# The opening of a fused two-block kernel: which queue and which engine prepare the first operands, and where the first norm factor is made

## The chip, the cores and the metric

The kernel runs on one NeuronCore of a Trainium2 chip. The metric is device time in microseconds (us) of one execution. The kernel before takes 1455.27 us, the median of three runs (1454.86 to 1456.52). The names of the engines in the profile are PE (TensorE, with its weight loads as PEld), DVE (VectorE), ACT (ScalarE), POOL (GpSimd) and SP (SyncE, which only issues transfers here).

## The reference

One sequence of 512 positions passes through two layers of width 1024. The change touches only the start of the first one:

```
h = rms_norm(x, g_mix)             # x * rsqrt(mean(x*x) + 1e-6) * g_mix
proj = h @ w_in                    # 1024 x 4352
u_a = proj[..., :1280]             # conv of 4 taps, two-way RG-LRU, @ p_a
u_b = proj[..., 1280:2304]         # pooled means, block-diagonal map, @ p_b
gates = sigmoid(proj[..., 2304:] + b_gate)
x = x + (gates[..., :1024] * y_a + gates[..., 1024:] * y_b) @ w_out
# then rms_norm, w_up, conv of 3 taps, gelu gate, w_down, and the second layer
```

Everything is float32. Channels lie on the 128 partitions and the 512 positions along the row, so x is eight tiles of 128x512.

## The kernel before, in words

**Three passes for each product.** A float32 operand is split into a rounded half "hi" and the remainder "lo". A block of the product (128 input channels times 128 output channels, 512 positions) is three matmuls: hi weights on hi data (L725), lo weights on hi data (L726), hi weights on lo data (L728). The function `block` (L715 to L731) issues them.

**Units of weights.** The weights lie in memory in the order of use, in units of eight blocks (128x1024, 512 KB). A unit goes through four steps: a load into `raw` (SP's queue, or ACT's for unit 1), the rounded half `whi` (ACT, L1222), the negative remainder `wlo` (ACT, L1231), and an accumulating transfer on GpSimd's queue that adds `raw` to it (L2544). For units 0, 1 and 2 VectorE makes the remainder instead, by one subtraction (`remainder`, L1730). `raw`, `whi` and `wlo` each have four slots.

**The first product starts before the norm is known.** The first four output tiles (two of the LRU's input, two of the pooled branch) are computed from v1 = x * g_mix, without the factor 1/rms, by `first`: for each of eight input tiles kk, one block of each of the four outputs. So units 0 to 3 are used up there, two kk to a unit. `gained(m)` (ACT, L1283) makes the hi half of v1's tile m, `gained_rest(m)` (DVE, L1724) the lo half. Both need g_mix, which is the first transfer on ACT's queue (L1275).

**The norm factor.** Squares of x are made on DVE and ACT and added up on DVE. Column sums on TensorE (`sums`, L780, eight small matmuls at a time in the profile) come in two parts: for tiles 0 to 3 after block (3, 1) and for tiles 4 to 7 after block (4, 2); (kk, n) is input tile kk, output n. ACT takes the root (L1246), DVE the reciprocal (L1678), and `to_rows(1)` (L845) after block (5, 0) spreads the factor over 128 partitions with four matmuls. From there DVE makes the normed tiles h1 (L1757), ACT their hi halves (L1307) and DVE their lo halves (L1683). All products behind `first` use h1. Then DVE scales the four outputs of `first` by the factor (L1769) and goes on with the conv and the recurrence.

**Before any operand is there** TensorE multiplies a tile of ones 17 times (`keep_warm_by_ones(17)`, L834), 34 matmul records in the profile.

Each engine runs its list in the order in which it is written, and waits at semaphores; the lists are written out by hand. `Units.due` says at which block a unit is due, which is why `weights(16)` on ACT in the opening stands for unit 4 alone, the first unit behind `first`.

Of the kernel before, what the change touches and what calls it, by code (L numbers as in the profile page):

```python
# [107 lines left out]
class Book:  # L108
# [107 lines left out]
class Kit:  # L216


    def __init__(self, nc, top, x_d, w_d, mod_d, cond_d, vec_d, cst_d, edge_d, ssm_d, uk_d, spill_d,
# [29 lines left out]
        self.gain_in, self.raw_part = sig("gain_in", 16), sig("raw_part", 16)  # L249
# [47 lines left out]
    def sb(self, *name):  # L297
        return self.place(*self.book.home[name])[0]
# [393 lines left out]
def tensor_engine(k, T):  # L692
# [21 lines left out]
    def block(tile, kk, pair, out, start, stop):  # L714

        u, j = divmod(len(k.plan), UB)
        k.plan.append((tile[0], kk, tile[1]))
        c = slice(128 * j, 128 * j + 128)
        wh, wl = k.whi[:, u % NHI, c], k.wlo[:, u % NLO, c]
        if u == 0 and j == 0:  # L720
            T.wait_ge(at("w_hi_part"), at("w_lo_part"))
        elif j == 0 or (u, j) == (0, UB // 2):
            T.wait_ge(at("w_hi", u), at("w_lo", u))
        T.wait_ge(at(pair, kk, "hi"))
        matmul(out, wh, sr(pair, kk, "hi"), start=start, stop=False)  # L725
        matmul(out, wl, sr(pair, kk, "hi"), start=False, stop=False)  # L726
        T.wait_ge(at(pair, kk, "lo"))
        mm = matmul(out, wh, sr(pair, kk, "lo"), start=False, stop=stop)  # L728
        if stop or j == UB - 1:
            mm.then_inc(*done.tick(tile if stop else None))  # L730
        if j == UB - 1:  # L731
            done.note("unit", u)
# [105 lines left out]
    def to_rows(n, copy=None):  # L838
# [5 lines left out]
        for t in range(4):  # L844
# [4 lines left out]


    T.wait_ge(at("ones"))
    keep_warm_by_ones(17)
    first(FIRST_IN, "v1", {(3, 1): lambda: sums([1], 0, last=4), (4, 2): lambda: sums([1], 4, last=4),
                           (5, 0): lambda: to_rows(1)})
    done.release(*[("v1", m, h) for m in range(8) for h in ("hi", "lo")])


# [353 lines left out]
def scalar_engine(k, A):  # L1211
# [22 lines left out]
    def weights(n):  # L1234
        rounded_weights(units.due(n))
# [36 lines left out]
            if m in between:  # L1272
                between[m]()

    A.eng.dma_start(k.vec[:, 0:8], k.vec_d[:, 0:8]).then_inc(*k.gain_in.tick(("gain",)))  # L1275
    A.eng.dma_start(k.raw[:, 0, 0:512], k.w_d[0][:, 0:512]).then_inc(*k.raw_part.tick(("raw_part",)))
    A.eng.dma_start(sb("x0", 1), k.x_d[1]).then_inc(*k.x_in[1].tick(("x0", 1)))
    A.eng.dma_start(k.raw[:, 1, :], k.w_d[1]).then_inc(*k.raw_in[1].tick(("raw", 1)))
    A.eng.preload_act_table(ACT.Sqrt)

    def gained(m):
# [2 lines left out]
            *done.tick(("v1", m, "hi")))  # L1284

    gained(0)
    A.wait_ge(at("raw_part"))
    act(k.whi[:, 0, 0:512], k.raw[:, 0, 0:512], ACT.Copy).then_inc(*k.w_hi.tick(("w_hi_part",)))
    A.wait_ge(at("raw", 0))
    act(k.whi[:, 0, 512:1024], k.raw[:, 0, 512:1024], ACT.Copy).then_inc(*k.w_hi.tick(("w_hi", 0)))  # L1290
    gained(1)
    gained(2)
    rounded_half(1)
    gained(3)
    rounded_weights([2])
    gained(4)
# [1 line left out]
        square(1, m, sb("x0", m), ("x0", m))  # L1298
    rounded_weights([3])
    gained(5)  # L1300
    root(1, 1024)
    gained(6)
    gained(7)
    weights(16)
    for m in range(8):
        A.wait_ge(at("nf", 1, m), *freed("h1", m, "hi"))
        act(sr("h1", m, "hi"), sb("nf", 1, m), ACT.Copy).then_inc(*done.tick(("h1", m, "hi")))  # L1307
        if m in (1, 3):
            weights(8)
# [346 lines left out]
def vector_engine(k, V):  # L1656
# [70 lines left out]
    def remainder(u, cols, raw, hi, lo):  # L1727
# [2 lines left out]
        tt(k.wlo[:, u, cols], k.raw[:, u, cols], k.whi[:, u, cols].bitcast(F32),  # L1730
           ALU.subtract).then_inc(*done.tick(lo))

    gained_rest(0)
    square(1, 0, sb("x0", 0), ("x0", 0))
    remainder(0, slice(0, 512), ("raw_part",), ("w_hi_part",), ("w_lo_part",))
    remainder(0, slice(512, 1024), ("raw", 0), ("w_hi", 0), ("w_lo", 0))
    square(1, 1, sb("x0", 1), ("x0", 1))
    gained_rest(1)
    gained_rest(2)
    square(1, 2, sb("x0", 2), ("x0", 2))  # L1740
    remainder(1, slice(0, 1024), ("raw", 1), ("w_hi", 1), ("w_lo", 1))
# [790 lines left out]
def gpsimd_engine(k, P):  # L2532
# [117 lines left out]
def sync_engine(k, Q):  # L2650
# [377 lines left out]
```

## Time and profile before

| | |
|---|---|
| median of 3 runs | 1455.27 us |
| the profiled execution | 1457.31 us, span 1456.0 us |
| PE busy | 1444.1 us (99%) |
| PEld busy | 1186.3 us (81%) |
| DVE, ACT busy | 886.3 us (61%), 785.8 us (54%) |
| first real matmul | 6.91 us after the span's start |
| mean granted TensorE clock | 0.999 |

A busy PE is read with care: matmuls overlap, so 99% says that PE has nearly always one in flight. What counts here is which of PE's stretches of idleness exist, and on which chain of work they hang. Times in the rows are from the start of the span. "From issue to landing" counts from the start of the issuing instruction.

### The profile page before, as it was taken

The numbers are of one execution on the slowest core, as the hardware profiler recorded it, in microseconds if no ns is written. First come the engines' busy times: TensorE is split into PE (matmuls) and PEld (weight loads), VectorE is DVE, ScalarE is ACT, GpSimd is POOL, SyncE is SP. The second block draws the span as 40 slices with busy tenths as digits, with TensorE's granted clock in tenths as the row PEclk, the third lists the DMA queues.
The fourth block names the chain that finished last, engine by engine and source line by source line (L and its number), as shares of the span: only waits on it lengthen the run. The fifth ranks groups of instructions, "written<-read, shape, count | busy, mean of one in ns | idle before, by whom it ended". The sixth has DMA issues, their size and how long they took to land.

```text
span 1456.0 us, 18322 instructions
## 1 busy us (share of the span) xinstructions
PE 1444.1 (99%) x6992; PEld 1186.3 (81%) x6992; DVE 886.3 (61%) x1624; ACT 785.8 (54%) x1081; POOL 168.9 (12%) x182
## 2 busy tenths in 40 slices
PE   9999999999999999999999999999999999999998
PEld 8887888888888888878888877776878888888887
DVE  7889754365695859376478667847866443333332
ACT  6698898745665647453444565597356222322221
POOL 1111111111111111100002421111010000000000
PEclk9999999999999999999999999999999999999999
DMA  8886877899999998783348666896468333333321
GB/s 247 200 194 164 205 192 198 195 323 294 304 250 250 253 236 221 189 266 118 108 166 280 201 160 166 204 338 218 152 159 228 134 116 102 87 108 98 98 72 58
DMA packets 86792, 274.90 MB, mean 189 GB/s; under 512 B 10081, under 2 KB 14433, under 8 KB 86705
## 3 DMA queue, kind: packets, MB, share of 16 engines
q1 hardware_dynamic: 62256, 190.95, 38.9%
q0 software_dynamic: 21200, 77.15, 27.6%
q10 hardware_dynamic: 3248, 5.64, 1.1%
q8 instruction: 55, 0.90, 0.2%
q14 instruction: 33, 0.26, 0.0%
HBM read 177.62 MB, written 17.83 MB: 134 GB/s over the span
## 4 chain that ended last, share of the span: by engine, by line
PE 82%; DVE 7%; ACT 7%; DMA 2%; issue 1%; SPq 0%; DVEq 0%; ACTq 0%
PE ps L725 25%; PE ps L728 25%; PE ps L726 25%; DMA wlo<-raw 1%; ACT whi L1222 1%; ACT wlo L1231 1%; DVE pl_r L1683 1%; ACT pl_f L1345 1%; DMA tab<-pl_f 1%; DVE pl_f L1814 1%; ACT pl_f L1541 1%; PE ps L960 0%; PE ps L979 0%; PE ps L1071 0%; DVE pl_f L2143 0%
## 5 line engine op out<-in xcount | busy, mean ns | idle before, releaser
L725 PE MATMUL ps<-pl_r,whi 128*128 128x512 f32 x1954 | 765.9, 392 | 5.3 <-DMA wlo<-raw 3.0
L728 PE MATMUL ps<-pl_r,whi 128*128 128x512 f32 x1954 | 760.8, 389 | 0.1
L726 PE MATMUL ps<-pl_r,wlo 128*128 128x512 f32 x1954 | 760.5, 389 | 0.0
L725 PEld LDWEIGHTS ps<-pl_r,whi 128*128 128x128 f32 x1954 | 366.9, 188 | 87.6 <-issue 7.4
L728 PEld LDWEIGHTS ps<-pl_r,whi 128*128 128x128 f32 x1954 | 366.8, 188 | 78.3 <-DVE pl_r L1683 0.9
L726 PEld LDWEIGHTS ps<-pl_r,wlo 128*128 128x128 f32 x1954 | 366.9, 188 | 74.8 <-issue 0.5
L1222 ACT ACTIVATE whi<-raw 128x1024 fp32r<-128x1024 f32 x246 | 259.1, 1054 | 174.7 <-PE ps L728 149.0
L2544 POOL DMA_DIRECT2D wlo<-raw x147 | 126.0, 857 | 836.3 <-ACT wlo L1231 822.0
L2232 DVE TENSOR_TENSOR wlo<-raw,whi 128x1024 fp32r<-128x1024 f32 x97 | 120.0, 1242 | 93.7 <-ACT whi L1222 93.7
L1231 ACT ACTIVATE wlo<-raw 128x1024 fp32r<-128x1024 f32 x147 | 153.8, 1046 | 0.0
L2498 DVE TENSOR_TENSOR pl_f<-ps,pl_f 128x512 f32<-128x512 f32 x20 | 13.8, 692 | 133.2 <-PE ps L728 133.2
L1683 DVE TENSOR_TENSOR pl_r<-pl_f,pl_r 128x512 fp32r<-128x512 f32 x112 | 77.2, 690 | 8.9 <-ACT pl_r L1251 4.9
L1251 ACT ACTIVATE pl_r<-pl_f 128x512 fp32r<-128x512 f32 x34 | 21.5, 632 | 112.6 <-DVE pl_f L2498 93.1
L1409 ACT ACTIVATE pl_f<-ps,vec 128x512 f32<-128x512 f32 x44 | 34.0, 775 | 67.8 <-PE ps L728 61.7
L2120 DVE CUSTOM_DVE_ANT_0 pl_f<-pl_f,pl_f 128x1024 f32<-128x1024 f32 x48 | 59.9, 1262 | 3.8 <-ACT pl_f L1383 3.8
L1241 ACT ACTIVATE pl_f<-pl_f 128x512 f32<-128x512 f32 x36 | 22.3, 627 | 63.3 <-DVE pl_f L2462 44.4
L1625 ACT ACTIVATE pl_f<-ps 128x512 f32<-128x512 f32 x20 | 11.9, 597 | 57.8 <-PE ps L728 57.8
L2646 POOL TENSOR_TENSOR pl_f<-pl_f,pl_f 128x256 f32<-128x256 f32 x2 | 1.4, 720 | 344.3 <-ACT pl_f L1648 344.3
L2194 DVE SCALAR_TENSOR_TENSOR pl_f<-ps,vec,pl_f 128x511 f32<-128x511 f32 x44 | 32.7, 744 | 10.0 <-ACT pl_f L1409 10.0
L1668 DVE TENSOR_TENSOR pl_f<-pl_f,pl_f 128x512 f32<-128x512 f32 x34 | 23.5, 693 | 20.2 <-ACT pl_f L1241 19.0
L2061 DVE TENSOR_TENSOR pl_f<-pl_f,lams 128x640 f32<-128x640 f32 x4 | 3.3, 824 | 52.3 <-DMA tab<-pl_f 52.3
L2197 DVE SCALAR_TENSOR_TENSOR pl_f<-ps,vec,pl_f 128x511 f32<-128x511 f32 x44 | 33.0, 750 | 1.6
(300 smaller groups left out, 1186.1 us busy)
## 6 DMA issues: line engine op xcount, KB each, us to landing
raw<-in_w SPq DMA_DIRECT2D x245, 512.0 KB, 4.6
wlo<-raw POOLq DMA_DIRECT2D x147, 512.0 KB, 7.1
pl_f<-in_mod SPq DMA_DIRECT2D x48, 512.0 KB, 7.8
pl_f<-tab SPq DMA_DIRECT2D x12, 512.0 KB, 6.9
xs<-pl_f SPq DMA_DIRECT2D x16, 256.0 KB, 6.5
tab<-pl_f SPq DMA_DIRECT2D x8, 512.0 KB, 6.5
pl_f<-xs SPq DMA_DIRECT2D x16, 256.0 KB, 5.9
spill<-pl_f ACTq DMA_DIRECT2D x16, 256.0 KB, 4.5
```

The source lines that it names most:

```text
L725: matmul(out, wh, sr(pair, kk, "hi"), start=start, stop=False)
L726: matmul(out, wl, sr(pair, kk, "hi"), start=False, stop=False)
L728: mm = matmul(out, wh, sr(pair, kk, "lo"), start=False, stop=stop)
L1222: act(k.whi[:, u % NHI, :], k.raw[:, u % NRAW, :], ACT.Copy).then_inc(*k.w_hi.tick(("w_hi", u)))
L1231: act(k.wlo[:, u % NLO, :], k.raw[:, u % NRAW, :], ACT.Copy, scale=-1.0).then_inc(*k.w_neg.tick(("w_neg", u)))
L1409: act(sb("up", j), ps("w_up", j), ACT.Identity, bias=vc("conv_f_b", j), scale=vc("conv_f_w", 44 + j)).then_inc(*done.tick(("up_tap", j)))
L1683: tt(sr(pair, m, "lo"), src, sr(pair, m, "hi").bitcast(F32), ALU.subtract).then_inc(*done.tick((pair, m, "lo"), *freed_by))
L2120: V.eng.tensor_tensor_reduce(r, r, sb(*c), 1.0, 0.0, ALU.mult, ALU.add, sm("mod", u)).then_inc(*done.tick(("mod_used", u), *([mod_home(u)] ...
L2194: stt(f[:, 1:S], b[:, 0:S - 1], vc("conv_f_w", j), f[:, 1:S], ALU.mult, ALU.add).then_inc(*done.tick())
L2197: stt(f[:, 0:S - 1], b[:, 1:S], vc("conv_f_w", 88 + j), f[:, 0:S - 1], ALU.mult, ALU.add).then_inc(*done.tick(("up", j), ("w_up", j)))
L2232: tt(k.wlo[:, u % NLO, :], k.raw[:, u % NRAW, :], k.whi[:, u % NHI, :].bitcast(F32), ALU.subtract).then_inc(*done.tick(("w_lo", u)))
L2544: P.eng.dma_start(k.wlo[:, u % NLO, :].bitcast(F32), k.raw[:, u % NRAW, :], accum_op=ALU.add).then_inc(*k.w_lo[u % NLO].tick(("w_lo", u)))
```

## The change

1. g_mix is no longer ACT's first transfer. GpSimd's queue carries it, ahead of the identity tile.
2. ACT's queue now starts with the first half of unit 0, then x's tile 1, then the first half of unit 1. The second half of unit 1 comes by SP's queue, behind the second half of unit 0. Before, unit 1 was one transfer on ACT's queue.
3. The hi part of the first half of unit 0 is made by VectorE (a cast) instead of ACT. VectorE does this and its remainder before `gained_rest(0)`.
4. The four blocks of kk = 0 go pass by pass (`begin`): four times hi on hi, four times lo on hi, four times hi on lo, with a wait ahead of each group in place of one ahead of all.
5. Unit 1 is rounded in two halves on ACT, and its remainder made in two halves on VectorE.
6. The warm-up has 10 products of ones in place of 17.
7. ACT's root comes behind `gained(5)` to `gained(7)` and unit 4's rounding (`weights(16)`), VectorE's reciprocal behind `gained_rest(7)`. On TensorE the sums go to (3, 3) and (5, 0), and `to_rows(1)` to (5, 3).

```diff
@@ tensor_engine @@
+    def begin(tiles, pair):
+        outs = [take(*t) for t in tiles]
...
+        T.wait_ge(at("w_hi_part", 0), at(pair, 0, "hi"))
+        for b, c in zip(outs, cols):
+            matmul(b, k.whi[:, 0, c], sr(pair, 0, "hi"), start=True, stop=False)
+        T.wait_ge(at("w_lo_part", 0))
+        for b, c in zip(outs, cols):
+            matmul(b, k.wlo[:, 0, c], sr(pair, 0, "hi"), start=False, stop=False)
+        T.wait_ge(at(pair, 0, "lo"))
+        for b, c in zip(outs, cols):
+            matmul(b, k.whi[:, 0, c], sr(pair, 0, "lo"), start=False, stop=False)
...
-    keep_warm_by_ones(17)
-    first(FIRST_IN, "v1", {(3, 1): lambda: sums([1], 0, last=4), (4, 2): lambda: sums([1], 4, last=4),
-                           (5, 0): lambda: to_rows(1)})
+    keep_warm_by_ones(10)
+    first(FIRST_IN, "v1", {(3, 3): lambda: sums([1], 0, last=4), (5, 0): lambda: sums([1], 4, last=4),
+                           (5, 3): lambda: to_rows(1)}, begin(FIRST_IN, "v1"))
@@ scalar engine @@
-    A.eng.dma_start(k.vec[:, 0:8], k.vec_d[:, 0:8]).then_inc(*k.gain_in.tick(("gain",)))
...
-    A.wait_ge(at("raw_part"))
-    act(k.whi[:, 0, 0:512], k.raw[:, 0, 0:512], ACT.Copy).then_inc(*k.w_hi.tick(("w_hi_part",)))
...
-    rounded_half(1)
...
-    root(1, 1024)
     gained(6)
     gained(7)
     weights(16)
+    root(1, 1024)
@@ vector engine @@
+    V.wait_ge(at("raw_part", 0))
+    copy(k.whi[:, 0, 0:512], k.raw[:, 0, 0:512]).then_inc(*done.tick(("w_hi_part", 0)))
+    remainder(0, slice(0, 512), ("raw_part", 0), ("w_hi_part", 0), ("w_lo_part", 0))
     gained_rest(0)
...
-    inverse(1)
     gained_rest(6)
     gained_rest(7)
+    inverse(1)
@@ gpsimd engine @@
+    P.eng.dma_start(k.vec[:, 0:8], k.vec_d[:, 0:8]).then_inc(*k.gain_in.tick(("gain",)))
     P.eng.dma_start(k.ident, k.cst_d[0]).then_inc(*k.ident_in.tick(("ident",)))
@@ sync engine @@
     dma(k.raw[:, 0, 512:1024], k.w_d[0][:, 512:1024]).then_inc(*k.raw_in[0].tick(("raw", 0)))
+    dma(k.raw[:, 1, 512:1024], k.w_d[1][:, 512:1024]).then_inc(*k.raw_in[1].tick(("raw", 1)))
```

How the lists move is seen best in the lists themselves. First, TensorE's opening before: one wait stands ahead of the first block and covers v1's halves and both halves of the weights (`pl_r_1_58` and `pl_r_1_60` are hi and lo of v1's tile 0).

```order
L834 MATMUL ps<-cst 128x128 [waits barrier_Pool_Activation_PE_DVE_SP_release,dve_done]
L834 MATMUL ps<-cst 128x128 x16
L725 MATMUL ps<-pl_r_1_58,whi 128x512 [waits act_done,dve_done,w_hi]
L726 MATMUL ps<-pl_r_1_58,wlo 128x512
L728 MATMUL ps<-pl_r_1_60,whi 128x512
```

And TensorE's opening after the change:

```order
L851 MATMUL ps<-cst 128x128 x9
L753 MATMUL ps<-pl_r_1_58,whi 128x512 [waits act_done,dve_done]
L753 MATMUL ps<-pl_r_1_58,whi 128x512 x3
L756 MATMUL ps<-pl_r_1_58,wlo 128x512 [waits dve_done]
L756 MATMUL ps<-pl_r_1_58,wlo 128x512 x3
L759 MATMUL ps<-pl_r_1_60,whi 128x512 [waits dve_done]
L759 MATMUL ps<-pl_r_1_60,whi 128x512 x3
```

The single wait is split in three, and the first of them no longer covers the remainder of the weights or the lo half of v1.

Second, TensorE around the norm factor, in kk = 5, whose hi and lo data are `pl_r_1_82` and `pl_r_1_84` before and `pl_r_1_80` and `pl_r_1_82` after. Before, from the first block of kk = 5 on:

```order
L725 MATMUL ps<-pl_r_1_82,whi 128x512 [waits act_done]
L726 MATMUL ps<-pl_r_1_82,wlo 128x512
L728 MATMUL ps<-pl_r_1_84,whi 128x512 [waits dve_done]
L845 MATMUL ps<-cst,sml 128x128 [waits ident_in,dve_done]
L845 MATMUL ps<-cst,sml 128x128 x3
L725 MATMUL ps<-pl_r_1_82,whi 128x512
```

After, from behind the first block of kk = 5 on (the sums of tiles 4 to 7 stand there now):

```order
L797 MATMUL ps<-cst,pl_f_1_83 128x1 x4
L726 MATMUL ps<-pl_r_1_80,whi 128x512
L727 MATMUL ps<-pl_r_1_80,wlo 128x512
L729 MATMUL ps<-pl_r_1_82,whi 128x512
L726 MATMUL ps<-pl_r_1_80,whi 128x512
L727 MATMUL ps<-pl_r_1_80,wlo 128x512
L729 MATMUL ps<-pl_r_1_82,whi 128x512
L726 MATMUL ps<-pl_r_1_80,whi 128x512
L727 MATMUL ps<-pl_r_1_80,wlo 128x512
L729 MATMUL ps<-pl_r_1_82,whi 128x512
L862 MATMUL ps<-cst,sml 128x128 [waits ident_in,dve_done]
L862 MATMUL ps<-cst,sml 128x128 x3
```

`to_rows` stood behind the first block of kk = 5 and now stands behind the fourth: three blocks, nine matmuls of 512 columns, are executed ahead of it that came behind it.

Third, ACT at the same place. Before, the root (`sml<-ps`) comes behind `gained(5)`:

```order
L1283 ACTIVATE pl_r_1_82<-pl_f_1_151,vec 128x512
L1246 ACTIVATE sml<-ps 128x4 [waits pe_done]
L1283 ACTIVATE pl_r_1_86<-pl_f_1_193,vec 128x512
L1283 ACTIVATE pl_r_1_90<-pl_f_1_165,vec 128x512
L1222 ACTIVATE whi<-raw 128x1024 [waits raw_in0]
L1231 ACTIVATE wlo<-raw 128x1024
L1307 ACTIVATE pl_r_1_74<-pl_f_1_139 128x512 [waits dve_done]
```

After:

```order
L1301 ACTIVATE pl_r_1_80<-pl_f_1_151,vec 128x512
L1301 ACTIVATE pl_r_1_86<-pl_f_1_193,vec 128x512
L1301 ACTIVATE pl_r_1_90<-pl_f_1_165,vec 128x512
L1239 ACTIVATE whi<-raw 128x1024 [waits pe_done,raw_in0]
L1248 ACTIVATE wlo<-raw 128x1024
L1263 ACTIVATE sml<-ps 128x4 [waits pe_done]
L1326 ACTIVATE pl_r_1_74<-pl_f_1_139 128x512 [waits dve_done]
```

The two activations of v1 and unit 4's two passes have changed places with the root.

## Rows read from the trace of the kernel before

**Rows 1.** The waits of PE over the whole span: released by: total, times, longest.

```profile
PE ps L725 <- DMA wlo<-raw: 3.0, 2, 1.8
```

**Rows 2.** Timeline of the first 8 us: start, duration, engine, line [idle before].

```profile
0.74 0.42 ACTq L1275 DMA_DIRECT2D vec<-in_vec  x1
3.93 0.72 ACT L1283 ACTIVATE pl_r<-pl_f,vec 128x512 fp32r<-128x512 f32 x1
4.79 0.75 DVE L1724 SCALAR_TENSOR_TENSOR pl_r<-pl_f,vec,pl_r 128x512 fp32r<-128x512 f32 x1 [3.79 <-ACT pl_r L1283]
5.03 0.63 ACT L1288 ACTIVATE whi<-raw 128x512 fp32r<-128x512 f32 x1 [0.38 <-DMA raw<-in_w]
6.07 1.28 DVE L1730 TENSOR_TENSOR wlo<-raw,whi 128x512 fp32r<-128x512 f32 x2
6.91 0.48 PE L725 MATMUL ps<-pl_r,whi 128*128 128x512 f32 x1
```

**Rows 3.** Line 834: ns min/median/max, starts; then stretches: length, busy (number), clock, DMA.

```profile
L834 PE MATMUL ps<-cst x34: 275/421/582, 1.1 to 6.9; 128*128 128x128 f32 x34
...
4.75:5.00 0.25, 0.25 (x3) 1.00 1.03 385
6.00:6.25 0.25, 0.25 (x5) 1.00 1.11 410
```

**Rows 4.** Transfers issued in the first 12 us: count, size, us to landing.

```profile
cst<-in_cst POOLq DMA_DIRECT2D x1, 64.0 KB, 4.1
vec<-in_vec ACTq DMA_DIRECT2D x1, 4.0 KB, 3.0
```

**Rows 5.** Packets of GpSimd's queue from 4.2 to 4.5 us: number, MB, share.

```profile
q0 software_dynamic: 13, 0.05, 42.9%
```

**Rows 6.** GpSimd's first transfer and two accumulating ones in the timeline.

```profile
1.27 0.73 POOL L2554 DMA_DIRECT2D cst<-in_cst  x1 [0.83 <-POOLq L3022]
16.71 0.87 POOL L2544 DMA_DIRECT2D wlo<-raw  x1 [14.71 <-ACT wlo L1231]
25.47 0.84 POOL L2544 DMA_DIRECT2D wlo<-raw  x1 [7.88 <-ACT wlo L1231]
```

**Rows 7.** Line 2544, landing, stretches 16 to 17, then 25 to 26 us.

```profile
DMA to landing us min/median/max: 8.7/8.7/8.7
...
DMA to landing us min/median/max: 6.4/6.4/6.4
```

**Rows 8.** The chain of waits where it leaves PE and returns: start, us, what.

```profile
23.36 0.91 PE ps L845 x8
24.26 0.02 issue
24.29 1.42 DVE pl_f L1757 x2
...
161.04 0.46 PE ps L725
```

**Rows 9.** Timeline of PE where a block begins or PE had waited.

```profile
24.00 0.47 PE L725 MATMUL ps<-pl_r,whi 128*128 128x512 f32 x1
26.17 0.39 PE L725 MATMUL ps<-pl_r,whi 128*128 128x512 f32 x1
31.99 0.47 PE L725 MATMUL ps<-pl_r,whi 128*128 128x512 f32 x1 [0.21 <-issue]
122.21 0.50 PE L725 MATMUL ps<-pl_r,whi 128*128 128x512 f32 x1 [0.86 <-DVE pl_f L1814]
144.00 0.47 PE L725 MATMUL ps<-pl_r,whi 128*128 128x512 f32 x1 [1.76 <-DMA wlo<-raw]
```

**Rows 10.** Timeline of DVE and ACT, 19 to 42 us.

```profile
19.29 0.74 DVE L1724 SCALAR_TENSOR_TENSOR pl_r<-pl_f,vec,pl_r 128x512 fp32r<-128x512 f32 x1
...
24.13 1.05 ACT L1231 ACTIVATE wlo<-raw 128x1024 fp32r<-128x1024 f32 x1
34.27 1.47 DVE L1683 TENSOR_TENSOR pl_r<-pl_f,pl_r 128x512 fp32r<-128x512 f32 x2
41.22 0.43 DVE L1689 CAST pl_r<-pl_f 128x512 fp32r<-128x512 f32 x1
```

More of the change, by code:

```diff
@@ L248, in __init__ @@
         self.cond_in = sig("cond_in", 16)
-        self.gain_in, self.raw_part = sig("gain_in", 16), sig("raw_part", 16)
+        self.gain_in = sig("gain_in", 16)
+        self.raw_part = [sig(f"raw_part_{u}", 16) for u in range(2)]
         self.vec_in, self.ident_in, self.tri_in, self.edge_in = (
@@ L719, in block @@
         wh, wl = k.whi[:, u % NHI, c], k.wlo[:, u % NLO, c]
-        if u == 0 and j == 0:
-            T.wait_ge(at("w_hi_part"), at("w_lo_part"))
-        elif j == 0 or (u, j) == (0, UB // 2):
+        if (u, j) == (1, 0):
+            T.wait_ge(at("w_hi_part", u), at("w_lo_part", u))
+        elif j == 0 or (u, j) in ((0, UB // 2), (1, UB // 2)):
             T.wait_ge(at("w_hi", u), at("w_lo", u))
@@ L743, in tile, with first @@
         give(w, m)
-    def first(tiles, pair, between={}):
-        outs = []
-        for kk in range(8):
+    def begin(tiles, pair):
+        outs = [take(*t) for t in tiles]
+        cols = [slice(128 * n, 128 * n + 128) for n in range(len(tiles))]
+        k.plan += [(t[0], 0, t[1]) for t in tiles]
+        T.wait_ge(at("w_hi_part", 0), at(pair, 0, "hi"))
[7 more added lines that the diff above has]
+            matmul(b, k.whi[:, 0, c], sr(pair, 0, "lo"), start=False, stop=False)
+        return outs
+    def first(tiles, pair, between={}, outs=()):
+        outs = list(outs)
+        for kk in range(1 if outs else 0, 8):
             for n, t in enumerate(tiles):
@@ L1273, in normed @@
                 between[m]()
-    A.eng.dma_start(k.vec[:, 0:8], k.vec_d[:, 0:8]).then_inc(*k.gain_in.tick(("gain",)))
-    A.eng.dma_start(k.raw[:, 0, 0:512], k.w_d[0][:, 0:512]).then_inc(*k.raw_part.tick(("raw_part",)))
+    A.eng.dma_start(k.raw[:, 0, 0:512], k.w_d[0][:, 0:512]).then_inc(
+        *k.raw_part[0].tick(("raw_part", 0)))
     A.eng.dma_start(sb("x0", 1), k.x_d[1]).then_inc(*k.x_in[1].tick(("x0", 1)))
-    A.eng.dma_start(k.raw[:, 1, :], k.w_d[1]).then_inc(*k.raw_in[1].tick(("raw", 1)))
+    A.eng.dma_start(k.raw[:, 1, 0:512], k.w_d[1][:, 0:512]).then_inc(
+        *k.raw_part[1].tick(("raw_part", 1)))
     A.eng.preload_act_table(ACT.Sqrt)
@@ L1291, in scalar_engine @@
     gained(1)
+    A.wait_ge(at("raw_part", 1))
+    act(k.whi[:, 1, 0:512], k.raw[:, 1, 0:512], ACT.Copy).then_inc(*k.w_hi.tick(("w_hi_part", 1)))
+    A.wait_ge(at("raw", 1))
+    act(k.whi[:, 1, 512:1024], k.raw[:, 1, 512:1024], ACT.Copy).then_inc(*k.w_hi.tick(("w_hi", 1)))
     gained(2)
-    rounded_half(1)
     gained(3)
@@ L1731, in remainder @@
            ALU.subtract).then_inc(*done.tick(lo))
+    V.wait_ge(at("raw_part", 0))
+    copy(k.whi[:, 0, 0:512], k.raw[:, 0, 0:512]).then_inc(*done.tick(("w_hi_part", 0)))
+    remainder(0, slice(0, 512), ("raw_part", 0), ("w_hi_part", 0), ("w_lo_part", 0))
     gained_rest(0)
+    remainder(0, slice(512, 1024), ("raw", 0), ("w_hi", 0), ("w_lo", 0))
     square(1, 0, sb("x0", 0), ("x0", 0))
-    remainder(0, slice(0, 512), ("raw_part",), ("w_hi_part",), ("w_lo_part",))
-    remainder(0, slice(512, 1024), ("raw", 0), ("w_hi", 0), ("w_lo", 0))
+    gained_rest(1)
+    remainder(1, slice(0, 512), ("raw_part", 1), ("w_hi_part", 1), ("w_lo_part", 1))
     square(1, 1, sb("x0", 1), ("x0", 1))
-    gained_rest(1)
+    remainder(1, slice(512, 1024), ("raw", 1), ("w_hi", 1), ("w_lo", 1))
     gained_rest(2)
     square(1, 2, sb("x0", 2), ("x0", 2))
-    remainder(1, slice(0, 1024), ("raw", 1), ("w_hi", 1), ("w_lo", 1))
     gained_rest(3)
```

## The prediction, made before the changed kernel was run

> **What bounds the kernel now.** I read the waits of PE first, since PE is busy 99% of the span. The reader is to see how little there is to win: the largest is 3.0 us for lo halves of weights, in two waits [rows 1]. So the opening is worth at most what lies ahead of the first real matmul at 6.91 us [rows 2], unless it moves something that PE waits for later. For that I read the chain of waits. It leaves PE at 24.26 us, when the norm factor is spread over the rows, goes on in VectorE and ScalarE, and comes back to PE only at 161.04 us [rows 8]. PE's own waits of 0.86 us at 122 us and 1.76 us at 144 us hang on that second chain [rows 9]. So for the first 161 us there are two clocks to watch: when PE starts, and when the factor is there. The second decides.
>
> **What sets PE's start before.** It is double. The warm-up is 34 records from 1.1 us on; slow ones last 421 ns, fast ones 275 ns. Number in a stretch times spacing is stretch plus duration: (250 + 421) / 3 gives a start every 0.22 us at first, (250 + 275) / 5 one every 0.105 us later [rows 3]. For all 34 to fit ahead of 6.9 us, about 21 must be slow. So the first ten products, 20 records, end at about 5.4 us, just where the pace rises, and the last seven are the 1.5 us behind. The remainder of the first half unit is the first of two subtractions that take 1.28 us from 6.07 us on, so it is done at 6.7 us [rows 2]. Both go: the remainder is made earlier, and seven products are dropped.
>
> **What is late next.** The first pass needs the hi half of v1's tile 0, for which ACT needs g_mix. Before, that took 3.0 us from an issue at 0.74 us [rows 2, 4]; ACT began at 3.93 us, took 0.72 us, and VectorE took the result up 0.14 us later [rows 2]. After, g_mix stands where the identity tile stood, at 1.27 us on GpSimd's queue [rows 6]. The identity took 4.1 us [rows 4], so it landed at 5.37 us; packets of that queue are seen from 4.2 us on [rows 5]. g_mix has the same 128 rows, with 32 bytes in each. Low end: as quick as on ACT's queue, 1.27 + 3.0 = 4.3 us. High end: twice the identity tile's 1.2 us from first packet to landing, 4.2 + 2.4 = 6.6 us, if many small packets between two full queues take their turn one by one. I take 5.5 us, since the identity tile is by far the nearest row. To PE's start that adds 0.72 us on ACT and 0.2 us of take-up: 6.4 us, between 5.4 us (the ten products end) and 7.5 us. PE starts 0.5 us earlier, at the ends 1.5 us earlier or 0.6 us later.
>
> The Trainium skill ("DMA: Bandwidth & Descriptors", section "Latency and other measured facts") gives about 0.6 us to the first byte on a hardware queue and about 1 us on GpSimd's. By it g_mix would land 0.4 us behind the low end, an estimate of 4.7 us. The trace speaks against it, with 2.9 us from GpSimd's first issue to its first packets.
>
> **What hides the rest.** The cast on VectorE is 0.43 us [rows 10], the subtraction behind it 0.64 us. VectorE was idle for 3.79 us there, and the half unit, which ACT took up at 5.03 us, moves one place forward on its queue [rows 2]. Cost nothing; if the cover went, 1.1 us on PE's start. Passes in groups of four use lo weights four matmuls and lo data eight matmuls behind the start, at 0.228 us each (below), and the lo half of v1 is done 0.9 us behind its hi half: no wait. Splitting unit 1 adds under 0.1 us to ACT and VectorE. VectorE's list up to the lo half of tile 5 ended at 20.03 us [rows 10], 13.1 us behind PE's start; with the two units' pieces regrouped I count 14.1 us from its `gained_rest(0)`, which begins as PE starts, and PE needs that result 14.9 us behind its start (five kk of 2.73 us, one set of sums of 0.8 us, two matmuls). It holds by under a microsecond. Unit 3's lo half was issued at 16.71 us and took 8.7 us [rows 6, 7], landing at 25.4 us for a use at 26.17 us [rows 9]; all ahead of it on ACT moves with PE's start or waits for loads. It holds too.
>
> **Unit 4.** It was issued at 25.47 us and took 6.4 us [rows 6, 7], so it landed at 31.87 us, and PE stood 0.21 us until 31.99 us [rows 9]. Ahead of the root it is issued some 5 us earlier. PE wins 0.2 us, if nothing else is late there.
>
> **The factor.** Something else is. `to_rows` has three blocks more ahead of it. Three blocks took from 24.00 to 26.17 us [rows 9], of which 0.12 us is a restart: 2.05 us, 0.228 us a matmul. The sums ahead of it are as many. ACT's root and VectorE's reciprocal fit beside these blocks and don't set it. The second chain therefore starts at 24.29 [rows 8] - 0.5 + 2.05 = 25.84 us, 1.55 us later. Its order is unchanged: unit 4's rounding ended at 24.13 + 1.05 = 25.2 us [rows 10], as the first h1 tile was made, so moving it takes nothing out of the chain, and units 5 and 6 stay in the h1 loop. The last lo half of h1 was done at 34.27 + 1.47 = 35.74 us [rows 10] and now comes at 37.3 us. PE, which would come to it at 31.78 - 0.5 + 23 x 0.228 = 36.5 us, loses 0.9 us in the first tile behind `first`, and ends it 0.2 us later than before. At 122 us it stands 0.86 + 1.3 = 2.2 us, at 144 us and 161 us as before. From there PE goes on alone, 1.5 us late.
>
> **Sum.** Start -0.5, unit 4 -0.2, first h1 tile +0.9, at 122 us +1.3: +1.5 us, which is the shift of the second chain. The profiled execution took 1457.31 us with a span of 1456.0 us, so it would be 1458.8 us; it stood 2.0 us over the median of the runs, and against these the forecast is 1455.27 + 1.5 = 1456.8 us. With the two ends of g_mix the shift is +0.55 or +2.65 us: 1455.8 to 1457.9 us. A measurement of this kernel can tell about 0.2% from no change, which is 2.9 us. So I forecast no change that can be told, with a lean to slower.
>
> **Rivals.**
>
> *The second chain has slack* (20%). The chain is inferred and has pieces called "issue"; if ScalarE waits in some of them for loads or units that PE releases, the 1.5 us is taken up on the way. Then the time follows PE: -0.5 - 0.2 us, 1454.6 us. For it: ACT's rounding waits for units that PE has used up. Against it: between 24.26 and 161.04 us the chain never passes through PE [rows 8], and PE's three waits there are all for the others.
>
> *GpSimd's queue is quick* (10%). g_mix lands near 4.3 us, PE starts at 5.4 us, the second chain moves by -1.5 + 2.05: +0.55 us, 1455.8 us. For it: 4 KB against 64 KB. Against it: the first packet was late, not only the last [rows 5]. By the skill's figures above the start would be an estimate of 5.6 us and the time 1456.0 us.
>
> *Slower: the clock comes up late* (10%). The granted clock reads 1.00 in these stretches, but the products of ones went at half pace until about 5.3 us, 4.2 us after PE's first work [rows 3]; half pace is that of 1.2 GHz, the later one that of 2.4 GHz. The ten products end where the pace rose, and behind them PE is idle for about 1 us. If the rise is lost and PE needs the same 4.2 us of work again, half of these, 2.1 us, are lost, and both chains start later by that: 1.5 + 2.1 = +3.6 us, 1458.9 us. It decides (over 2.9 us) from 2.8 us at half pace. For it: before, nothing idle stood ahead of the rise. Against it: 1.76 us of idleness at 144 us [rows 9] left PE at full pace. The Trainium skill ("TensorE: Matmul & The Clock Gate", section "Part 1: The HAM clock gate (the "warmup" mystery)") says that the gate samples recent activity without regard to the kernel's start; by that the rise could shift from run to run, which no row here shows.
>
> *The rest* (5%): VectorE's list or unit 3's transfer runs past my count and PE stands some 0.5 us more ahead of `to_rows`, 1457.3 us.
>
> **How the numbers follow.** Forecast 55%, at 1456.8 us. The range takes in the slack case and the ends of g_mix and stops short of the late clock: 1454.3 to 1458.3 us. Faster by over 0.2% (under 1452.4 us) would need more than PE's own 1.7 us at the best: 2%. Slower by over 0.2% (over 1458.2 us) is the late clock: 10%. Within: 88%.
>
> **What would show it.** PE's first real matmul at 6.4 us, with `gained(0)` on ACT at 5.5 us, released by a transfer; at 5.4 us the quick queue was right. The first `gained_by_factor` on VectorE at 25.8 us. A wait of about 0.9 us of PE for lo halves in the first tile of h1, and none for unit 4. PE's wait at 122 us over 2 us. If PE's return at 161 us is earlier than before, the slack case was right. If the first twelve real matmuls take over 4 us in place of 2.7 us, it was the clock. I am wrong altogether if VectorE's chain starts before 24.3 us, or the time falls by over 2 us.

## The result, and the profile after

| | before | after |
|---|---|---|
| median | 1456.04 us (8 runs, 1454.86 to 1457.23) | 1459.56 us (8 runs, 1458.68 to 1461.4) |
| ratio, 95% interval | | 1.0024 [1.0015, 1.0033] |
| profiled execution | 1457.31 us, span 1456.0 us | 1459.23 us, span 1457.9 us |

The change makes the kernel 3.5 us slower (2.2 to 4.8 us by the interval), which lies outside the forecast range. In the text below "+1.3 us" stands for the median of an experiment less the median of the kernel before, whose runs took turns with it on one chip; the interval of such a difference is about 1.3 us to either side.

The first 8 us of the profile after, as in [rows 2] (start, duration, engine, line [idle before]):

```profile
1.28 0.73 POOL L2576 DMA_DIRECT2D vec<-in_vec  x1 [0.84 <-POOLq L3046]
4.69 0.43 DVE L1753 CAST whi<-raw 128x512 fp32r<-128x512 f32 x1 [3.68 <-DMA raw<-in_w]
5.15 0.69 DVE L1749 TENSOR_TENSOR wlo<-raw,whi 128x512 fp32r<-128x512 f32 x1
6.14 0.72 ACT L1301 ACTIVATE pl_r<-pl_f,vec 128x512 fp32r<-128x512 f32 x1 [2.71 <-DMA vec<-in_vec]
7.01 1.17 PE L753 MATMUL ps<-pl_r,whi 128*128 128x512 f32 x4 [1.33 <-ACT pl_r L1301]
```

The weights are ready at 5.84 us, ahead of g_mix, so they are hidden as forecast; but g_mix lands at 6.1 us, not at 5.5 us. PE starts 0.1 us later than before, not 0.5 us earlier. The transfer from issue to landing, to be held against [rows 4]:

```profile
vec<-in_vec POOLq DMA_DIRECT2D x1, 4.0 KB, 4.8
```

Next, where the second chain starts on VectorE, and the waits of PE behind it, from the timeline ([rows 8, 9] have them before: 24.29 us, 0.86 us, 1.76 us):

```profile
26.44 1.41 DVE L1779 SCALAR_TENSOR_TENSOR pl_f<-pl_f,vec,ps 128x512 f32<-128x512 f32 x2 [2.72 <-PE ps L862]
...
55.37 0.47 PE L726 MATMUL ps<-pl_r,whi 128*128 128x512 f32 x1 [0.53 <-DMA wlo<-raw]
124.23 0.50 PE L726 MATMUL ps<-pl_r,whi 128*128 128x512 f32 x1 [1.25 <-DVE pl_f L1836]
145.89 0.47 PE L726 MATMUL ps<-pl_r,whi 128*128 128x512 f32 x1 [1.65 <-DMA wlo<-raw]
201.69 0.47 PE L726 MATMUL ps<-pl_r,whi 128*128 128x512 f32 x1 [0.40 <-DMA wlo<-raw]
```

The chain is 2.15 us late: the 0.1 us of the start and the 2.05 us of the three blocks. The wait for unit 4 at 31.99 us [rows 9] is gone.

The bracket shows the idle time only. PE's stream loses about 0.25 us more at each such wait: without one the next of these matmuls starts 0.23 us behind the last, while the idle time is counted from the last one's end, 0.39 us behind its start, and the first matmul after a wait takes longer. So the 0.53 us at 55.37 us is 0.8 us by the starts of the matmuls, against the same matmuls of before. Where "late" is said below of PE's stream, it is meant in this way.

Two waits are new and stood in no step of mine, 0.53 us at 55.37 us and 0.40 us at 201.69 us, both for an accumulating transfer of GpSimd's. They are small here, and they are the thread to the cause.

### The profile page after: what moved, and what is told of

Same layout as the page of the kernel before. It is cut to its first block, busy times and chain, and to the rows that moved or that the text cites. A ratio compares the mean times of both kernels' runs of the same rounds, so it can differ in the third digit from the quotient of the medians.

```text
span 1457.9 us, 18300 instructions
## 1 busy us (share of the span) xinstructions
PE 1444.6 (99%) x6978; PEld 1185.8 (81%) x6978; DVE 886.9 (61%) x1626; ACT 785.2 (54%) x1081; POOL 169.3 (12%) x183
## 4 chain that ended last, share of the span: by engine, by line
PE 85%; ACT 7%; DVE 4%; DMA 2%; issue 1%; DVEq 0%; ACTq 0%; POOLq 0%
PE ps L726 27%; PE ps L729 26%; PE ps L727 26%; DMA wlo<-raw 2%; ACT whi L1239 1%; ACT wlo L1248 1%; ACT pl_f L1364 1%; ACT pl_f L1560 1%; PE ps L1088 1%; PE ps L977 0%; PE ps L996 0%; DVE pl_f L2165 0%; PE ps L862 0%; ACT L1376 0%; ACT L1372 0%
## 5 line engine op out<-in xcount | busy, mean ns | idle before, releaser
L1258 ACT ACTIVATE pl_f<-pl_f 128x512 f32<-128x512 f32 x36 | 22.4, 627 | 62.4 <-DVE pl_f L2484 44.3
L1849 DVE SCALAR_TENSOR_TENSOR pl_f<-pl_f,pl_f 128x512 f32<-128x512 f32 x20 | 12.9, 688 | 33.0 <-ACT pl_f L1376 33.0
```

## The experiments

Lines are those of the kernel after where nothing else is said. The label of each run stands in bold.

### Half undone: the queue, the norm's order, the warm-up

**a1_again** is the changed kernel once more.

> The changed kernel once more, nothing edited. In its profile PE starts at 7.01 us (6.91 us before) and the normed tiles begin at 26.44 us (24.29 us before), and the span is 1.9 us longer; the timed runs were 3.5 us slower (2.2 to 4.8). Theory A (only these two shifts, the rest is scatter of the runs): the repeat comes out at +2 us, 1.4 to 2.8. Theory C (in many runs the idle time ahead of the first real matmul lets TensorE start at half pace, which the profiled execution happened not to show): again about +3.5 us, and a profile may show real matmuls of over 0.4 us spacing near 7 us.

Measured: 1460.54 us against 1456.33 us, ratio 1.0027 [1.0017, 1.0038], +4.2 us. Its profile has what the profile after has not. PE's first blocks, from the timeline:

```profile
7.05 2.04 PE L753 MATMUL ps<-pl_r,whi 128*128 128x512 f32 x4 [1.35 <-ACT pl_r L1301]
8.89 1.91 PE L756 MATMUL ps<-pl_r,wlo 128*128 128x512 f32 x4
10.59 1.14 PE L759 MATMUL ps<-pl_r,whi 128*128 128x512 f32 x4
```

Four matmuls of 512 columns took 2.04 us in place of 1.17 us: until 10.7 us PE ran at the pace of 1.2 GHz, and was 1.8 us late by 12.5 us. So the late clock of my rival exists, in some executions. I took it for the cause.

**a4_warm17** gives the seven products back.

```diff
-    keep_warm_by_ones(10)
+    keep_warm_by_ones(17)
```

> The changed kernel with 17 warm-up products as before, which end at about 6.8 us, so that PE is not idle ahead of the first real matmul at 7.0 us. Theory A: no difference from the changed kernel in the same call. Theory C: about 1.5 us faster than it, and a smaller scatter of its runs.

Measured: 1457.60 us, ratio 1.0009 [1.0, 1.0017], +1.3 us. PE starts at 7.08 us at full pace, the second chain at 26.49 us. Against a1, run by turns with it, 2.9 us of the loss hang on seven products. I read that as the clock confirmed, which was rash: seven products are activity, and they are also 28 instructions.

**a3_norm_early** puts the sums to (3, 1) and (4, 2), `to_rows` to (5, 0), the root behind `gained(5)` and the inverse behind `gained_rest(5)`, as before.

> The changed kernel with the sums, the root, the reciprocal and to_rows where the kernel before has them; g_mix stays on GpSimd's queue. Theory A: PE starts at 7.0 us and the normed tiles begin at 24.4 us, 2.05 us earlier than in the changed kernel: +0.1 us against the kernel before, PE waits at 122 us 0.9 us again. Theory C: the same shift of the normed tiles, but 1.5 us of half pace stays: +1.6 us. If the second chain had slack, taking 2 us off it would change nothing: +2 to +3.5 us.

Measured: 1458.78 us, ratio 1.0017 [1.0008, 1.0026], +2.4 us. Here the warm-up ended at full pace at 5 us, PE stood idle for 2 us, and the granted clock fell after it had risen. The stretches of PE (stretch, length, busy (number), granted clock, DMA share, GB/s):

```profile
7.00:8.00 1.00, 1.00 (x4) 0.72 1.07 412
8.00:9.00 1.00, 1.00 (x4) 0.50 1.08 426
9.00:10.00 1.00, 1.00 (x3) 0.50 1.00 408
10.00:12.00 2.00, 2.00 (x8) 0.79 1.05 417
```

0.50 is 1.2 GHz. That fall came behind idleness of 2 us at the start, where 1.76 us at 144 us [rows 9] had done nothing. PE was 1.6 us late by 12.5 us.

**a2_gain_on_act** issues g_mix first on ACT's queue again.

> The changed kernel with g_mix first on ACT's queue again; all else as changed. Theory A: g_mix lands near 3.7 us, ACT's first activation starts by 4.1 us, PE's first real matmul comes at about 5.4 us, where the ten warm-up products end. The normed tiles start 17.4 + 2.05 us behind that, at 24.9 us: +0.6 us against the kernel before, so 1.5 us faster than the changed kernel. Theory C: the idle time of PE ahead of the first real matmul is gone with it, so the gain over the changed kernel is larger, about 3 us, and the result +0.5 us too. A third view, that g_mix's queue doesn't matter because something else holds PE: no gain, +2 to +3.5 us.

Measured: 1459.60 us, ratio 1.0021 [1.0012, 1.003], +3.3 us. PE started at 5.50 us, at full pace, 1.5 us ahead of the changed kernel, and at most 0.9 us of it arrived (1459.60 us against 1460.54 us of a1). 0.7 us went at once, since x's tile 1 and the half unit behind g_mix on that queue came later (ACT waited 2.06 us for tile 1, until 7.49 us), and then there is this, from the timeline of PE and the list of transfers issued from 47 to 54 us:

```profile
57.20 0.47 PE L726 MATMUL ps<-pl_r,whi 128*128 128x512 f32 x1 [3.09 <-DMA wlo<-raw]
```

```profile
wlo<-raw POOLq DMA_DIRECT2D x2, 512.0 KB, 9.1
```

**b1_both_back** undoes both, with ten products.

> The changed kernel with g_mix first on ScalarE's queue and the norm's pieces at their old places; 10 warm-up products, halves and passes as changed. By the theory: TensorE starts at 5.5 us with an idle time of under 0.3 us ahead of it, so its clock comes up in time; the second chain at 23.6 to 23.9 us, 0.4 to 0.7 us ahead of before (0.7 us of the earlier start are lost again at x0[1], as in the run with g_mix alone); the end 0.4 to 0.7 us ahead of before, if the accumulating transfer behind the wait near 55 us lands as before; ratio 0.9996. Rival: what the early start brings is eaten by that wait, which has a deadline that moves with TensorE: then the time is that of before or 0.5 to 1 us over it, and the wait near 55 us is 1 us or more.

Measured: 1458.61 us, ratio 1.0018 [1.0009, 1.0027], +2.5 us: on the rival's side of my expectation, and more than its 0.5 to 1 us. PE started at 5.84 us at full pace, and its second chain at 25.09 us was only 0.8 us late. The wait at 55.19 us was 0.85 us, with 0.55 us at 201.59 us. The start was not late, the pace was full and the norm's order was that of before, so none of these is behind the 2.5 us here.

### The kernel before, with one part of the change

**b3_before_norm_late** has the norm's pieces at the changed places, in the kernel before.

> The kernel before with one part of the change alone: the sums, to_rows (three blocks later), the root behind unit 4 and the inverse behind the last tiles. By my step: the second chain 2.05 us later, at 26.3 us, TensorE's waits up to 37 us gone or under 0.5, and the end 1.2 to 2.1 us over before (ratio 1.0010 to 1.0014), some of it at the wait near 55 us. Rival, the slack that I gave 20%: the end within 0.5 us of before.

Measured: 1458.46 us against 1456.14 us, ratio 1.0013 [1.0004, 1.0022], +2.3 us, with the chain at 26.91 us (0.57 us of it from a later start). The three blocks cost time where I said. The size is over the 1.2 to 2.1 us that I expected, and takes in the later start, so 2.3 us is no measure of them alone.

**b2_before_gain_pool** has g_mix on GpSimd's queue, in the kernel before.

> The kernel before with one part of the change alone: g_mix's transfer ahead of the identity on GpSimd's queue. It lands at 6.05 us for 4.9 by the trace of the changed kernel, ScalarE makes tile 0's high half at 6.1 and the half unit's behind it at 6.8, and TensorE starts at 8.0 us (before 6.91); the second chain comes 1.1 us later, at 25.4. The 17 warm-up products then end about 1.5 us ahead of the start. If the idle time costs the clock here too, the first blocks run at half pace and the end is 2.0 to 3.5 us over before; if it doesn't, 0.6 to 1.1 us. If nothing of the first microseconds reaches the end, the time is that of before.

Measured: 1457.24 us, ratio 1.0008 [0.9999, 1.0016], +1.1 us, for a PE that started at 9.28 us, 2.4 us late, and a chain at 26.65 us. I had expected the start at 8.0 us; VectorE had two other tiles in hand ahead of the remainder of unit 0, which it began at 8.50 us. A chain over 2 us late costs 1.1 us at the medians, with an interval that reaches down to nothing, so some of it is taken up later. PE was idle for 1.78 us ahead of its start, and then ran at full pace.

### Nearly all of the change kept, and as fast as before

**c1_norm_early_warm17** joins the edits of a3_norm_early and a4_warm17.

> The changed kernel with two things as before had them: 17 warm-up products, and the sums, the root, the inverse and to_rows at their old places; g_mix stays on GpSimd's queue, and the halves and passes stay changed. If the loss is the idle TensorE ahead of its first blocks (about 2.9 us by the run with 17 products) plus the later second chain (the rest, about 1.3), nothing is left: the second chain at 24.4 to 24.6 us (before 24.29), the time within 0.6 us of before, ratio 1.000. If the work on units 0 and 1 costs something by itself, or 17 products alone took the whole of the loss that the order did not, 1.3 us or more over before stays.

Measured: 1455.64 us, ratio 1.0001 [0.9992, 1.001], -0.5 us; chain at 24.75 us. The halves, the passes, the cast on VectorE and g_mix's queue together cost nothing that can be told. **d3_rows** has also the second sums and `to_rows` one block earlier.

> The run with 17 warm-up products and the norm's pieces at their old places (1455.64), with the second sums and to_rows one block earlier. VectorE's last square for them ended at 20.4 us there, TensorE would ask at 20.7: no wait. Second chain at 24.06 (24.75 there, before 24.29); the end 0.2 to 0.7 us under that run, 1455.2, if the chain decides; the same 1455.6 if the end is set by the transfers behind it alone.

Measured: 1455.49 us, ratio 1.0001 [0.9992, 1.001], -0.2 us: no gain that can be told. It and c1 are the nearest to a better version that the runs found. **d1_gain_sp** has c1's order, 11 products, and g_mix first on SyncE's queue; **d2_gain_sp_rows** adds the block of d3.

> The changed kernel with the norm's pieces at their old places, 11 warm-up products, and g_mix first on SyncE's queue, ahead of tile 0: neither GpSimd's queue carries it nor ScalarE's, where it held up x0[1] and the half unit. Tile 0 is issued 0.45 us later, lands near 4.9 us, and TensorE starts at 5.6 us (changed kernel 7.01, before 6.91) with under 0.3 us of idle ahead. x0[1] and the half unit 1 are there by 7.3 and 7.9 us as in the changed kernel. Expected: second chain at 23.6 to 24.0 us (before 24.29), 0.3 to 0.7 us ahead at the end, 1455.6, ratio 0.9996. Rival: three transfers at once at the start hold each other up as in the run with both back (x0[1] at 7.6, half unit at 9.0), the second chain at 25 us and the time 2 us over before.

> As the run before it, and the second sums one block earlier and to_rows one block earlier (0.69 us). If the second chain alone sets what follows, it comes at 23.1 us and the end is 0.3 to 0.7 us ahead of the run before it. If VectorE's squares are not done by then, TensorE waits at the sums by the same 0.5 us, and nothing is gained.

Measured: 1458.53 and 1457.83 us, ratios 1.0019 [1.001, 1.0028] and 1.0014 [1.0005, 1.0023], +2.8 and +2.1 us. PE started at 6.24 and 6.39 us, at full pace, and the chains came at 25.27 and 24.55 us, not at the 23.6 to 24.0 and 23.1 us that I expected: PE waited for VectorE near 10 and 17.5 us, 1.0 us together in each kernel. d2 and c1 have the same chain within 0.2 us and 2.6 us between them.

### What divides the kernels

Laid side by side, the profiles fall into two groups, by the number of warm-up products. Of all instruction packets of queue q8 (16 KB each), the one near 45 us, and the accumulating transfer that PE asks for near 54 us:

| | packet q8 starts | issue to landing | PE's wait there |
|---|---|---|---|
| 17 products: before, a4, b2, b3, c1, d3 | 41.9 to 44.3 us | 5.1 to 7.3 us, median 6.3 us | 0 to 0.05 us |
| 10 or 11: after, a1, a2, a3, b1, d1, d2 | 48.1 to 52.6 us | 6.9 to 9.4 us, median 8.0 us | 0.4 to 3.1 us |

The transfer is issued at 46 to 50 us, so in the second group the packet falls on it. The trace records each of its 16 parts as it lands: in a2 fifteen are there from 53.0 to 54.4 us and the last at 57.06 us, in b1 fifteen by 53.65 us and the last at 55.05 us; with 17 products all 16 are there within 1.2 us. The gap between the last part and the one before it is 0.4 to 2.7 us in every profile of the second group and at most 0.1 us in the first. A second packet stands at 196 to 199 us in the second group, shortly ahead of the wait near 201 us, and at 188 to 191 us in the first; the last part of a transfer is 1.1 to 1.8 us behind the others near 201 us in the second group, at most 0.1 us in the first. The packet of the queue and the transfer issued from 48 to 50 us, after:

```profile
q8 instruction: 1, 0.02, 4.5%
wlo<-raw POOLq DMA_DIRECT2D x1, 512.0 KB, 6.9
```

And before, from 41 to 44 us:

```profile
q8 instruction: 1, 0.02, 1.9%
```

That q8 carries TensorE's code is worked out from the page of the profile and not shown outright: `q8 instruction: 55, 0.90, 0.3%` beside 6978 matmuls and as many weight loads is 0.90 MB for 13956 instructions, about 64 bytes each, 256 to a packet. In before two packets stand at 72.4 and 101.8 us, 29.4 us apart, which is the time of 129 matmuls with their weight loads, 258 instructions. Seven products have two records of each kind each: 28 instructions, a ninth of a packet.

**e2_before_wide10** and **e3_norm_early_wide10** keep the columns and take the instructions: ten products of 218 columns (2180) for 17 of 128 (2176), in the kernel before and in c1. **e1_norm_early_again** is c1 once more.

```diff
-            mm = matmul(b[:, 0:128], k.ones, k.ones, start=True, stop=True)
+            mm = matmul(b[:, 0:218], k.ones, k.ones[:, 0:1].broadcast_to([128, 218]), start=True, stop=True)
```

> The changed kernel with the norm's pieces at their old places and 17 warm-up products, once more, as the yardstick of this call: 1455.6, 0.0 to 0.5 us under before, no wait near 55 us, the instruction packet at 43 us.

> The kernel before with 10 warm-up products of 218 columns for 17 of 128: the same columns, 28 instructions fewer. Theory of the code packet: TensorE starts at 6.9 us at full pace, the second chain stays at 24.3, the 16 KB packet moves from 42 us to 48 us, the accumulating transfer's last part lands 1 to 3 us behind the other 15, TensorE waits 0.5 to 2 us near 54 us, and the end is 0.7 to 2.0 us over before. Rival, that only the clock and the second chain count: the time of before within 0.3 us.

> The yardstick of this call with 10 warm-up products of 218 columns for 17 of 128. Theory of the code packet: start and second chain as in the yardstick, a wait of 0.5 to 3 us near 54 us, the end 1.0 to 2.5 us over it. Rival: its time within 0.3 us.

Measured: e1 1456.91 us, ratio 0.9998 [0.9989, 1.0007]; e3 1459.52 us, ratio 1.0020 [1.0011, 1.003]; before 1456.79 us. The intervals of e1 and e3 don't meet: 2.6 us lie between them. Both start at full pace (7.77 and 7.31 us) and have their chains at 25.16 and 24.78 us, the slower kernel's the earlier. PE's new waits in e3:

```profile
54.99 0.47 PE L726 MATMUL ps<-pl_r,whi 128*128 128x512 f32 x1 [0.96 <-DMA wlo<-raw]
...
201.32 0.47 PE L726 MATMUL ps<-pl_r,whi 128*128 128x512 f32 x1 [0.44 <-DMA wlo<-raw]
```

e2 came out smaller than I expected: 1457.39 us, ratio 1.0002 [0.9993, 1.0011], +0.6 us. Its packet moved to 49.6 us and its transfer took 7.5 us, but PE's wait was 0.30 us, and none at 201 us. The last part was late here too, 1.14 us behind the other 15, and PE's stream was 0.5 us later behind the wait than ahead of it. Whether the packet costs anything in the kernel before can't be told from the times of this run.

**e4_after_short17** turns it round: 17 products of 40 columns in the changed kernel.

> The changed kernel with 17 warm-up products of 40 columns for 10 of 128: about the columns of 10, the instructions of 17. Theory of the code packet: TensorE idle for 1 to 2 us ahead of its start and, in many executions, at half pace behind it, as in the changed kernel; yet no wait near 55 and 201 us: 1458.3 to 1459, 1 to 1.5 us under the changed kernel and still 2 to 3 over before. Rival, clock alone: the changed kernel's 1459.6 to 1460.5.

Measured: 1460.96 us, ratio 1.0029 [1.0019, 1.0039], +4.2 us. The packet went to 45.5 us and the waits to 0.30 us and none, as expected; but the kernel was no faster, since something else came in, in the profile at least. The short products took as long as long ones, the warm-up ran to the end at the slow pace, and PE started later and slow:

```profile
1.06 7.48 PE L851 MATMUL ps<-cst 128*128 128x40 f32 x34 [1.06 <-DVE cst L1732]
8.34 2.05 PE L753 MATMUL ps<-pl_r,whi 128*128 128x512 f32 x4
10.19 1.62 PE L756 MATMUL ps<-pl_r,wlo 128*128 128x512 f32 x4
```

It was 2.8 us late by 12.5 us, half of it by the start and half by the pace. With the packet off the transfer the last part was on time (0.01 us behind the one before), so the two go together in both directions; but the run does not settle what the packet costs. It shows that a late start with the late clock on top does reach the end: 2.9 us over a4_warm17's +1.3 us.

**f1_after_wide10** is the changed kernel with the wide products, **f2_warm17_again** a4 once more, on one chip.

> The changed kernel with 10 warm-up products of 218 columns for 10 of 128: activity up to TensorE's start as with 17 products, instructions as in the changed kernel. If the code packet carries the difference: packet at 48 to 51 us, waits near 55 and 201 us as in the changed kernel, 1459.3 to 1460.5 (3 to 4 us over before). If the late clock carries it: no half pace at the start, 1457.6, as f2.

> The changed kernel with 17 warm-up products of 128 columns once more, as the yardstick of this call: 1457.6, 1 to 1.6 us over before; packet at 43 us, no wait over 0.4 us near 55 us.

Measured, against 1456.08 us: f1 1459.82 us, ratio 1.002 [1.0011, 1.003], +3.7 us; f2 1457.52 us, ratio 1.001 [1.0001, 1.0018], +1.4 us. The start of f1, then of f2:

```profile
7.40 1.25 PE L753 MATMUL ps<-pl_r,whi 128*128 128x512 f32 x4
8.49 1.08 PE L756 MATMUL ps<-pl_r,wlo 128*128 128x512 f32 x4
```

```profile
7.02 1.16 PE L753 MATMUL ps<-pl_r,whi 128*128 128x512 f32 x4
8.02 1.07 PE L756 MATMUL ps<-pl_r,wlo 128*128 128x512 f32 x4
```

Both are at full pace, the idle time and the late clock are cured in f1, and it still has the changed kernel's time. The intervals of f1 and f2 just meet, but six of f1's ten runs are slower than the slowest of f2's eleven. What divides them, in f1 from 46 to 56 us (queues, then the transfers issued there, with the median us to landing) and at PE:

```profile
q8 instruction: 1, 0.02, 0.6%
wlo<-raw POOLq DMA_DIRECT2D x2, 512.0 KB, 7.3
```

```profile
56.59 0.47 PE L726 MATMUL ps<-pl_r,whi 128*128 128x512 f32 x1 [1.35 <-DMA wlo<-raw]
```

And f2, where the same stretch has no row of q8:

```profile
wlo<-raw POOLq DMA_DIRECT2D x2, 512.0 KB, 6.1
```

```profile
54.97 0.47 PE L726 MATMUL ps<-pl_r,whi 128*128 128x512 f32 x1 [0.19 <-DMA wlo<-raw]
```

### How much of it the waits account for

In the late order the wait near 55 us is given back at 124 us, where PE waits for the second chain anyway. f1, then f2:

```profile
125.04 0.50 PE L726 MATMUL ps<-pl_r,whi 128*128 128x512 f32 x1 [0.87 <-DVE pl_f L1836]
```

```profile
124.22 0.50 PE L726 MATMUL ps<-pl_r,whi 128*128 128x512 f32 x1 [1.65 <-DVE pl_f L1836]
```

How far PE's stream in the kernel with ten wide products is behind that of its partner with 17, by the starts of the same matmuls in the two profiles:

| | at 45 us | 60 us | 130 us | 210 us | 660 us | end |
|---|---|---|---|---|---|---|
| f1 less f2 | 0.5 | 1.6 | 0.8 | 0.8 | 1.7 | 1.6 |
| e3 less e1 | -0.4 | 0.8 | 0.7 | 1.5 | 0.9 | 0.9 |

So in the late order the waits near 55 and 201 us are worth 0.3 us in the end, and in the early order 1.9 us. The next step comes near 645 us, at a wait that the kernel before has as well; it is the second of the two waits in [rows 1]. Before, then f1:

```profile
643.54 0.47 PE L725 MATMUL ps<-pl_r,whi 128*128 128x512 f32 x1 [1.21 <-DMA wlo<-raw]
```

```profile
645.35 0.47 PE L726 MATMUL ps<-pl_r,whi 128*128 128x512 f32 x1 [0.60 <-DMA wlo<-raw]
```

Six of the ten profiles with ten or eleven products have it (0.6 to 2.1 us), and three of the eight with 17 of 128 columns. There the last part is not always the late one (0.03 us behind the others in before), so it is not shown to be the packet's work.

The clock bears on it too. In six profiles the granted clock fell to 1.2 GHz for 3.4 us between its rise and the last microseconds (a3 near its start, five near 1091 us), and exactly these six have a mean granted clock of 0.998 or less. That mean was taken of the timed runs too: 44 of 102 with ten or eleven products are at 0.998 or less, and 48 of 216 with 17 of 128 columns. Without them the medians of f1 and f2 lie 1.3 us apart (1458.79 and 1457.49 us), those of e3 and e1 1.1 us (1457.47 and 1456.40 us), from five to eight runs each. So about half of what the pairs show may come by more frequent falls of the clock; why they are more frequent no run shows.

## Why the prediction was wrong

**The step that failed is the sum's silence on the seven products.** I priced them as time ahead of PE's start ("the last seven are the 1.5 us behind") and as warmth, and not as code. Taken out at equal columns and full pace they cost 2.3 us in the changed order (f1 against f2) and 2.6 us in the old one (e3 against e1). The pairs differ in the number of instructions, and besides in the width of the products and in how these read the ones; no run separates these. That something behind the start costs over 2 us is shown. The late last part of the transfer goes with the packet in every profile. But the packet is not the whole account: the idle time near 55 and 201 us adds up to 0.4 to 3.3 us in these profiles (1.4 us in e3 and in f1), in f1 most of it is given back at 124 us, and the falls of the clock and the wait near 645 us take their part. In the kernel before the same step cost +0.6 us, which can't be told from nothing.

**The factor.** "2.05 us" for three blocks was right: the chain is 2.15 us late with the 0.1 us of the start. That all of it reaches the end was not. With 17 products the late pieces cost 1.3 and 1.4 us (a4, f2) where the early ones cost -0.5 and +0.1 us (c1, e1): 1.5 us. In b2 a chain 2.4 us late cost 1.1 us. Where the rest is taken up the profiles don't show: near 640 us they scatter by up to 2.2 us against each other in every order. The net +1.5 us of my sum was thus right by two errors: a chain 0.6 us later than I had it, and slack that I had given to a rival at 20%.

**PE's start.** -0.5 us was forecast and +0.1 us measured. The mis-sized term is g_mix's landing: 4.8 us from issue where I took 4.2 us, with the same 128 rows as the identity tile's 4.1 us [rows 4], and below my high end. The Trainium skill's figures ("DMA: Bandwidth & Descriptors", section "Latency and other measured facts"), with their estimate of 4.7 us for the landing, were off by 1.4 us.

**What hides the rest; unit 4.** Right: c1 has all of it and is as fast as before, and the wait for unit 4 is gone. It was worth 0.45 us and not 0.2 us, by the starts of the matmuls; the sum took the idle time for the loss.

**PE in the first h1 tile and at 122 us.** 0.9 us was forecast. PE was idle for 0.5 us (0.17 and 0.30 us, near 36 and 37 us), and its stream lost 1.2 us. At 124.23 us 2.2 us was forecast and 1.25 us measured, since PE had been stopped at 55 us by then; without that it waited 1.80 us (a4). The cause of both was right.

**Rivals.** The late clock gave 1458.9 us and came nearest to the number. Its mechanism is real: three of the profiles with the changed start had it or a fall of the clock (a1, a3, e4), at 1.4 to 1.7 us on PE. It is not needed for the changed kernel's time. Kept warm at the same instructions, the kernel took +3.7 us (f1) for +3.5 and +4.2 us, and in the old order +2.7 us (e3) for +2.4 us (a3); a share below about 1.3 us can't be told by this. Being near a number is no proof of a mechanism.

**The account.** 1.5 us for the norm's pieces and 2.3 to 2.6 us for the seven products are 3.8 to 4.1 us, for 3.5 and 4.2 us measured. What stays open: how the 2.3 to 2.6 us are shared among the packet, the falls of the clock and the wait near 645 us; and why 28 instructions, some 3.2 us of matmuls, move the packet by 5 to 10 us and not by 3.2 us.

## What to carry to other kernels

A product taken out of an engine's stream takes instructions with it, and here the later packets of the instruction queue moved against the transfers; where a kernel waits for transfers with half a microsecond to spare, change one at a time, and keep one variant with the same work and another number of instructions (here 10 x 218 columns against 17 x 128) as a control. Give back one suspected cause only if the edit gives back nothing else: the run that seemed to prove the clock changed two things. When several kernels with different starts all share a new wait far from the edit, look at what they have in common. Then add up where the streams of two kernels part, by the starts of the same instructions, and not the idle times alone: one wait can be given back at the next.

## What the hardware showed that I had not expected

- With one 16 KB packet of the instruction queue among the packets of a 512 KB accumulating transfer, 15 of its 16 parts landed close together and the last up to 2.7 us behind them (a2), in all ten profiles that have it there and in none of the others; the whole counts as landed only then.
- The clock's rise behind the start scatters at nearly the same work: PE's pace rose between 3.9 and 7.2 us in most profiles, at 10.7 us in a1, at 11.4 us in e4, and in a3 it rose at 4.0 us and fell again from 7.4 to 10.9 us.
- Products of 40 columns came at the same spacing as those of 128 (7.48 us for 34 records, 0.22 us each) at the slow pace, and didn't bring the pace up.
- 4 KB in 128 rows took 4.8 us on GpSimd's queue at the kernel's start, more than 64 KB on the same queue before (4.1 us).
- In five of 19 profiles (after, a2, d2, f1, f2) the granted clock fell to 1.2 GHz for 3.4 us between 1090 and 1097 us and cost 1.5 to 1.7 us. PE was busy when it fell, and had been idle for 0.7 to 0.8 us some 2.2 to 2.8 us earlier; the other 14 profiles have the same idle time there and no fall. By the mean granted clock of the timed runs such falls come about twice as often with ten or eleven products.
